# A two-block network on one core: the first 27 weight units in another order, and the taps of a 31-tap convolution summed in PSUM

## What is computed

```
u = rmsnorm(h, g_mix);  z = u @ w_in
zq, zkv, zg, zc, zm = split(z)               # queries, 6 x 2 groups of keys/values, gates, conv input, merge gates
kc, vc = compress(kv[0]), compress(kv[1])    # windows of 32 tokens, stride 16: gelu(flat(blocks + pos) @ w1) @ w2
o_c, o_s, o_w = attention of q over (kc, vc), (kv[2], kv[3]), (kv[4], kv[5])
y_a = (g0 * o_c + g1 * o_s + g2 * o_w) @ w_o_nsa     # g = sigmoid(zg)
c = c_val * sigmoid(c_gate)                  # the two halves of zc, 512 channels each
c = silu(layernorm(causal_dwconv(c, conv_w, conv_b)))       # 31 taps per channel
y_b = c @ w_conv_out + b_conv_out
h = h + (sigmoid(ga) * y_a + sigmoid(gb) * y_b) @ w_out
```

## Time and profile before

| | us |
|---|---|
| median of 3 runs | 2301.78 (2301.23 to 2301.85) |
| the profiled execution | 2300.76 |
| its span | 2298.8 |
| TensorE busy | 2156.7 (94%) |
| VectorE busy | 1082.4 (47%) |
| ScalarE busy | 863.0 (38%) |
| GpSimd busy | 925.4 (40%) |
| mean granted TensorE clock | 0.973 |

### The profile page before, as it was taken

The page is one execution under the profiler, slowest core; times in us unless marked ns, Lnnn a source line. Parts: engine busy times, 40 slices in busy tenths (PEclk is TensorE's granted clock), DMA queues, the critical chain, the costliest instruction groups (busy, mean ns, idle before and its releaser), DMA issues.

```text
span 2298.8 us, 25188 instructions
## 1 busy us (share of the span) xinstructions
PE 2156.7 (94%) x10138; PEld 1766.7 (77%) x10138; DVE 1082.4 (47%) x1665; ACT 863.0 (38%) x1344; POOL 925.4 (40%) x415
## 2 busy tenths in 40 slices
PE   7449999999999999989999999999899999999996
PEld 6437777778888888777777888888788788888875
DVE  3996666535552423556654423222553245222145
ACT  4123444434442335444443423223532234233243
POOL 4242222344444444522215444443654454444452
PEclk9779999999999999999999999999999999999998
DMA  4122111223333233211112233232223223333321
GB/s 151 55 92 65 47 45 48 73 92 102 101 92 101 93 105 105 64 56 56 46 37 93 92 101 101 92 101 92 93 71 103 90 75 101 93 100 97 96 90 49
DMA packets 53252, 192.73 MB, mean 84 GB/s; under 512 B 5904, under 2 KB 6032, under 8 KB 53136
## 3 DMA queue, kind: packets, MB, share of 16 engines
q1 hardware_dynamic: 52704, 189.55, 26.4%
q10 hardware_dynamic: 432, 1.57, 0.2%
HBM read 189.00 MB, written 2.10 MB: 83 GB/s over the span
## 4 chain that ended last, share of the span: by engine, by line
PE 82%; DVE 12%; ACT 5%; issue 1%; POOL 0%; DMA 0%; DVEq 0%; ACTq 0%; POOLq 0%
PE ps L461 25%; PE ps L463 24%; PE ps L462 24%; DVE conv_acc L1044 4%; PE ps L625 1%; PE ps L605 1%; PE ps L864 1%; ACT w_hi L1646 1%; DVE ps L1553 1%; PE ps L617 1%; PE ps L524 1%; PE ps L882 1%; DVE resid L1558 1%; DVE tile_a L1312 1%; PE ps L517 1%
## 5 line engine op out<-in xcount | busy, mean ns | idle before, releaser
L425 POOL TENSOR_TENSOR w_lo<-w_raw,w_hi 128x1024 fp32r<-128x1024 f32 x353 | 855.4, 2425 | 1303.8 <-ACT w_hi L1646 1303.8
L461 PE MATMUL ps<-xg_hi,w_hi 128*128 128x512 f32 x1776 | 712.1, 401 | 38.1 <-POOL w_lo L425 17.1
L463 PE MATMUL ps<-xg_hi,w_lo 128*128 128x512 f32 x1776 | 697.2, 393 | 0.0
L462 PE MATMUL ps<-xg_lo,w_hi 128*128 128x512 f32 x1776 | 697.0, 392 | 0.0
L1646 ACT ACTIVATE w_hi<-w_raw 128x1024 fp32r<-128x1024 f32 x353 | 372.7, 1057 | 623.6 <-PE ps L463 615.0
L461 PEld LDWEIGHTS ps<-xg_hi,w_hi 128*128 128x128 f32 x1776 | 336.8, 190 | 107.6 <-issue 22.2
L463 PEld LDWEIGHTS ps<-xg_hi,w_lo 128*128 128x128 f32 x1776 | 336.2, 189 | 71.7
L462 PEld LDWEIGHTS ps<-xg_lo,w_hi 128*128 128x128 f32 x1776 | 337.2, 190 | 63.9 <-issue 0.2
L462 PE MATMUL ps<-h_lo,w_hi 128*128 128x512 f32 x688 | 267.9, 389 | 0.0
L463 PE MATMUL ps<-h_hi,w_lo 128*128 128x512 f32 x688 | 267.9, 389 | 0.0
L461 PE MATMUL ps<-h_hi,w_hi 128*128 128x512 f32 x688 | 267.9, 389 | 0.0
(11 more groups left out here) (303 smaller groups left out, 2335.2 us busy)
## 6 DMA issues: line engine op xcount, KB each, us to landing
w_raw<-in_weights SPq DMA_DIRECT2D x353, 512.0 KB, 3.5
resid<-in_x SPq DMA_DIRECT2D x4, 512.0 KB, 6.9
out_x<-resid SPq DMA_DIRECT2D x8, 256.0 KB, 2.0
p_raw<-in_p ACTq DMA_DIRECT2D x3, 512.0 KB, 3.6
vec<-in_vectors SPq DMA_DIRECT2D x1, 252.5 KB, 4.3
```

Source lines behind the costliest of these rows:

```text
L425: pool.tensor_tensor(w_lo[:, slot, :], w_raw[:, u % RAW, :], w_hi[:, slot, :].bitcast(F32), ALU.subtract).then_inc(w_ready, 1)
L461: pe.matmul(o, w, x, start=start, stop=False)
L462: pe.matmul(o, w, xl, start=False, stop=False)
L463: return pe.matmul(o, wl, x, start=False, stop=stop)
```

## The change

- **Order of units**: `cmp_in` (4), `glu` tiles 0 to 3, then 8 pairs of one compression unit and one projection unit: `hidden_k` with `glu` tiles 4 to 7, `hidden_v` with the two keys and the two values. Then `q0`, `cmp_out`, `gates`. The packing of the weights follows. The group of five at the start is now `cmp_in` and the first `glu` tile.
- **Banks**: new ones for these units; the compression's sums lie in banks 4 and 5, its transposed hidden tiles both in bank 6, and both transposed value tiles, one after the other, in bank 3, so that the second transpose waits for `vv_lo` of the first (`s_kv["lo"]` of 4).
- **Taps**: the sum of every channel tile is in bank 7 (`taps(count)`). 62 lie ahead of attention in pieces of 2 to 14; 62 beside it, two in each slot, the second behind `pt_lo`. LayerNorm's additions move to the slots (0, 1), (4, 0) and (7, 3).
- **Gates**: their sigmoid goes into `ln_sum` instead of `sq`, and the transpose of the gates moves behind the first scores.
- **Start**: x in five pieces of 1, 1, 2, 2 and 2 chunks; ACT issues the 8 columns of `vec` with the first gain and the first half of unit 0, SP the second half; ACT and POOL split unit 0 by halves and TensorE starts on the first; the rest of `vec` comes behind x; a token activation stands ahead on ACT; TensorE multiplies `ones` by `ones` 8 times ahead of its first wait.
- `blk_lo` moves to another place in SBUF.

```diff
-    stage("glu", 8)
     stage("cmp_in", 4)
-    stage("cmp_hidden", 8)
-    stage("keys", 2)
+    stage("glu", 4)
+    stage("hidden_k", 8)
+    stage("hidden_v", 8)
+    stage("q0", 1)
     stage("cmp_out", 1)
-    stage("values", 2)
     stage("gates", 1)
-    stage("q0", 1)
...
+def glu_unit(t):
+    U = layout_units()
+    return U["glu"] + t if t < 4 else U["hidden_k"] + 2 * (t - 4) + 1
+def hidden_unit(kv, i):
+    return layout_units()[("hidden_k", "hidden_v")[kv]] + 2 * i
+def kv_unit(n):
+    return layout_units()["hidden_v"] + 2 * n + 1
...
+    for i in range(4):
+        bank[U["cmp_in"] + i] = i
+    for t in range(8):
+        bank[glu_unit(t)] = (4, 5, 6, 0, 1, 2, 3, 0)[t]
+    for n in range(4):
+        bank[kv_unit(n)] = (1, 2, 3, 0)[n]
+    bank[U["q0"]], bank[U["gates"]] = 2, 0
...
             load_x(0)
-            sp.dma_start(vec[:], vectors).then_inc(vec_loaded, 16)
-            load(0)
+            sp.dma_start(w_raw[:, 0, UW // 2:UW], weights[0, :, UW // 2:UW]).then_inc(w_loaded[0], 16)
             load_x(1)
+            load(1)
             load_x(2)
             load_x(3)
-            for u in range(1, U["end"]):
+            load_x(4)
+            sp.dma_start(vec[:, DC:NVEC], vectors[:, DC:NVEC]).then_inc(vec_loaded, 16)
+            for u in range(2, U["end"]):
...
+            for half in range(2):
+                cols = slice(half * UW // 2, (half + 1) * UW // 2)
+                pool.wait_ge(first_hi if half == 0 else w_hi_ready, 1)
+                pool.tensor_tensor(w_lo[:, 0, cols], w_raw[:, 0, cols], w_hi[:, 0, cols].bitcast(F32),
+                                   ALU.subtract).then_inc(first_ready if half == 0 else w_ready, 1)
...
+            pe.wait_ge(c_dve, 4)
+            for _ in range(EARLY_IDLE):
+                pe.matmul(ps[:, 0, 0:P], ones[:], ones[:], start=True, stop=True)
...
+            for t in range(1, 4):
+                unit(glu_unit(t))
+            for i in range(4):
+                hidden(0, i)
+                unit(glu_unit(4 + i))
+            for n in range(4):
+                hidden(1, n)
+                unit(kv_unit(n))
+                if n == 0:
+                    hidden_turn(0)
             hidden_turn(1)
-            unit(U["keys"] + 1)
+            values_turn(0)
+            unit(U["q0"])
+            values_turn(1)
...
+            def values_turn(j):
+                pe.wait_ge(bank_free, kv_unit(2 + j) + 1)
+                if j:
+                    pe.wait_ge(s_kv["lo"], 4)
...
+            def taps(count):
+                for n in range(tapped[0], tapped[0] + count):
                     ct, k = divmod(n, CONV_TAPS)
-                    acc, src, w = conv_acc[:, ct, :], glu[:, ct, k:k + S], vcol("conv_w", n)
-                    if ct == CT - 1:
-                        acc = ps[:, NB, :]
+                    acc, src, w = ps[:, NB, :], glu[:, ct, k:k + S], vcol("conv_w", n)
...
+            blocks(0, "pos_k")
+            glu_tile(0)
+            blocks(1, "pos_v")
+            block_low(0)
+            dve.wait_ge(bank_free, glu_unit(1) + 1)
+            taps(2)
+            block_low(1)
+            glu_tile(1)
+            taps(14)
+            glu_tile(2)
+            taps(14)
+            dve.wait_ge(bank_free, glu_unit(5) + 1)
+            glu_tile(3)
+            taps(4)
+            keys(0)
             hidden_low(0)
+            taps(6)
+            keys(1)
+            taps(8)
+            dve.wait_ge(bank_free, kv_unit(1) + 1)
+            kv_scaled(2, T2[:, 0:1, :])
+            taps(8)
+            kv_scaled(3, T2[:, 1:2, :])
             hidden_low(1)
+            taps(EARLY_TAPS - 56)
+            values_low(0)
+            query_scaled(0)
+            query_low(0)
+            values_low(1)
...
-                    if tap < CT * CONV_TAPS:
-                        taps(tap, tap + 1)
-                    elif tap < CT * CONV_TAPS + 3:
-                        ln_add(tap - CT * CONV_TAPS + 1)
+                    if tapped[0] < CT * CONV_TAPS:
+                        taps(1)
...
                         head_low(A1, event(b) + i, i)
+                    if tapped[0] < CT * CONV_TAPS:
+                        taps(1)
...
+            act.dma_start(vec[:, 0:DC], vectors[:, 0:DC]).then_inc(gain_loaded, 16)
+            act.dma_start(w_raw[:, 0, 0:UW // 2], weights[0, :, 0:UW // 2]).then_inc(first_loaded, 16)
+            act.wait_ge(c_dve, 4)
+            act.activation(token[:, 13:14], eps_col[:], ACT.Copy).then_inc(c_act, 1)
...
+            highs(glu_unit(0) + 1 + RING)
+            highs(glu_unit(1) + 1 + RING)
+            block_high(0)
+            glu_sigmoid(0)
+            highs(glu_unit(2) + 1 + RING)
+            block_high(1)
+            highs(glu_unit(3) + 1 + RING)
+            glu_sigmoid(1)
...
+            highs(kv_unit(0) + 1 + RING)
+            keys(0)
+            hidden_high(0)
+            highs(kv_unit(1) + 1 + RING)
+            keys(1)
```

More of the change, by code:

```diff
@@ L116, in bank_table @@
     bank = {}
[L117 to L121, removed]
+    for i in range(4):
[5 more added lines that the diff above has]
+    bank[U["q0"]], bank[U["gates"]] = 2, 0
+    for u in range(U["pairs"], U["w_out"]):
+        bank[u] = u % 2
     embeds = {U[f"ple{n}"] + i for n in range(3) for i in range(2)}
@@ L265, in build @@
             stat = sb("stat", [P, 3, 2, QB], scope=att)
+            with ExitStack() as early:
+                blk_lo = sb("blk_lo", [P, 2, 16, 2 * NC1], F32R, early)
             pt_hi = sb("pt_hi", [P, 2, S], F32R, att)
@@ L545, in _, with hidden @@
             group(u0, 7, DC, ready=prepared(0))
-            for u in range(u0 + GROUPS[u0], U["cmp_hidden"]):
-                unit(u)
+            def hidden(kv, i):
+                uu = hidden_unit(kv, i)
+                if i == 0:
+                    pe.wait_ge(s_cmp["lo"], kv + 1)
+                weights_here(uu)
+                for c in range(4):
+                    o = ps[0:2 * NC1, 4 + kv, 0:2 * P]
+                    xh, xl = blk_hi[:, kv, 4 * i + c, :], blk_lo[:, kv, 4 * i + c, :]
+                    wh, wl = (w[:, uu % RING, c * 2 * P:(c + 1) * 2 * P] for w in (w_hi, w_lo))
+                    mm = three(o, xh, wh, xl, wl, i == 0 and c == 0, i == 3 and c == 3)
+                mm.then_inc(unit_done, 1)
@@ L554, in hidden_turn @@
                 mm.then_inc(s_cmp["turned"], 1)
[L556 to L568, removed]
@@ L583, in _, with gates_turn @@
             mm.then_inc(unit_done, 1)
[L584 to L587, removed]
+            unit(U["gates"])
+            def gates_turn():
+                pe.wait_ge(s_gate["sig"], 1)
                 for tb in range(QB):
[L589 to L594, removed]
+                    mm = pe.transpose(ps[:, 4, tb * 32:(tb + 1) * 32], ln_sum[0:32, tb * P:(tb + 1) * P], ident[0:32, 0:32])
+                mm.then_inc(s_gate["turned"], 1)
             def head_scores(A, s, qi, terms):
@@ L1045, in taps, with glu_tile, blocks @@
                     ins.then_inc(s_mrg["conv"], 1)
[L1048 to L1051, removed]
+                tapped[0] += count
+            def glu_tile(i):
+                u, v = glu_unit(2 * i), glu_unit(2 * i + 1)
                 scaled(u, T[:, i % 2:i % 2 + 1, :], s_glu["t"])
-                scaled(u + 1, bank(u + 1), s_glu["t"])
+                scaled(v, bank(v), s_glu["t"])
                 dve.wait_ge(s_glu["t"], 2 * i + 2)
                 dve.wait_ge(s_glu["sig"], i + 1)
[L1056 to L1075, removed]
+                dve.tensor_tensor(glu[:, i:i + 1, PAD:PAD + S], T[:, i % 2:i % 2 + 1, :], bank(v), ALU.mult).then_inc(bank_free, 2 if i < 2 else 4)
+            def blocks(kv, pos):
                 for g in range(2):
@@ L1728, in _ @@
-            act.wait_ge(s_cmp["out"], 4)
-            copy_hi(kc_hi[:], kc_f[:], s_cmp["khi"])
-            copy_hi(vc_hi[:], vc_f[:], s_cmp["khi"])
-            highs(U["values"] + 2 + RING)
-            highs(U["gates"] + 1 + RING)
-            taken(U["gates"])
-            act.activation(sq[:, 0, :], T[:, 0, :], ACT.Sigmoid).then_inc(s_gate["sig"], 1)
+            values_high(0)
             def query_high(p):
@@ L1741, in _ @@
             query_high(0)
-            for j in range(2):
-                act.wait_ge(s_kv["turned"], j + 1)
-                for hd in range(2):
-                    cols = slice(hd * HD, (hd + 1) * HD)
-                    copy_hi(vv_hi[:, hd, j, :, cols], ps[:, 6 - j, :].rearrange("p (a b) -> p a b", b=P)[:, :, cols], s_kv["hi"])
+            values_high(1)
+            highs(U["cmp_out"] + 1 + RING)
+            act.wait_ge(s_cmp["out"], 4)
+            copy_hi(kc_hi[:], kc_f[:], s_cmp["khi"])
+            copy_hi(vc_hi[:], vc_f[:], s_cmp["khi"])
+            highs(U["gates"] + 1 + RING)
+            taken(U["gates"])
+            act.activation(ln_sum[:], T[:, 0, :], ACT.Sigmoid).then_inc(s_gate["sig"], 1)
             def exps(A, e, par, st, pr, qi, b):
```

197 lines of the change are left out of this document (112 added, 85 removed).

## The result

The changed kernel takes 2236.76 us (median of 4 runs, 2233.05 to 2239.36), the kernel before 2301.82 on the same chip: a ratio of 0.971 [0.968, 0.973], 65 us less. 2233.2 was forecast, in a range of 2223 to 2252. The profiled execution took 2233.05 us, the one before 2300.76: 67.7 less, where the sum of terms says 68.55. Runs of one kernel differ by 6 us here.

A forecast was written before the change was run, and what follows sets the result against it. VectorE's lateness ahead of attention, from convolution taps held beside POOL, was taken as the bound. Terms 5.4 + 62.3 + 7.05 - 3.8 - 0.9 - 1.5 = 68.55 us off 2300.76 gave 2232.2, plus 1.0 for the median: 2233.2 (2223 to 2252).

The forecast's parts named there:

- the check from below: Attention's start added up from TensorE's own items, first matmul to gates: 127.5 us, 70 earlier than 197.45.
- 1, the first matmul: Kernel start: first matmul at 7.0 us instead of 12.36, gain 5.4 us (4.5 to 6.5).
- 2, the waits: Ahead of attention, TensorE's waits on compression blocks' low parts, `hid_lo`, split weights, `tile_a` and `vv_lo` go: 62.3 us gained.
- C: Weight supply holds the unit pairs, as ACT takes splits behind sigmoids that wait for VectorE: 2243 us, chance 0.09.
- 3, the clock: Low-clock stretches behind waits ahead of attention go, half the start's too: gain 7.05 us (5 to 8), 0.85 at the start.
- 4, the new wait: Second value transpose: TensorE waits for `vv_lo` of the first, loss 3.8 us (0 to 7), plus 0.9 for low clock.
- 5, attention: Attention: 33 more taps beside it, delays taken up in the wait for `pt_hi`; loss 1.5 us (0 to 10).
- Two of the signs named: In attention: VectorE busy over 75%, and TensorE's waits not over 5 us.
- 6, gates and LayerNorm: Gates' sigmoid behind the first scores and LayerNorm's moved additions cost nothing; the sigmoid, if uncovered, 1 to 2 us.
- The rule weighed: VectorE competes with GpSimd only with two SBUF inputs or in a two-port mode; so early taps take 0.785 us.
- A: Early taps are held by POOL even with sums in PSUM, 25 us more on VectorE: 2258 us, chance 0.04.
- E: The mixed stage of short and long units never gets the high clock, slower than before: 2324 us, chance 0.02.

The follow-up runs named there:

- light second taps: The changed kernel with 29 of the 31 second taps in attention replaced by a one-element memset: 2232.64 us, 0.969 of the kernel before.

## Why the prediction was right, step by step

**The sum.** Up to attention the terms make 70.05 us and 67.8 came. Of the 2.2 missing, 2.1 stand at the end of the first group, 39.6 us where the check from below has 37.5: the first matmul was 0.6 late, and the group took 32.0 us and not 30.5. Attention took 3.3 us more, where the sum has 1.5. That the profiled execution still comes within 1 us of the sum is luck: behind attention, where nothing changed, it is 3.1 us shorter than the one before (TensorE is busy for 1811.8 us and not 1814.7, with the same 8316 matmuls). The changed kernel's second profile does not have these 3 us: 1876.0 there, against 1875.0 before and 1871.9 in the first.

**What bounds.** VectorE's lateness in the first stretch, and taps blocked beside POOL: shown from both sides, by one half of the change at a time.

**1, the first matmul.** 7.64, not 7.0; the gain is 4.7, inside 4.5 to 6.5 (8.15 in the second profile, and 7.7 to 8.1 in the experiments with this start). ACT had waited 0.46 us for the first half of unit 0 when it copied it at 5.45, and POOL had split it by 7.5. The working ended at 7.5, and the 0.5 that I took off for smaller pieces was not there: they landed at 5.4, not at 4.4.

**2, the waits.** 62.3 forecast, and all of it went. No unit behind the first one waits for weights up to attention, against C. C's mechanism is real all the same: with the taps in SBUF it is where most of the lateness comes out (15.6 us).

**3, the clock.** The four stretches behind waits went. At the start I counted 0.85 gained, and 1.0 was lost: 13 low matmuls in the profile (8 in the second one), where before has 8. The step asked whether a pause of 2 us would lose the high level; in this execution the eight idle matmuls never reached it. With 13 of them the first eviction comes 2.6 us earlier (1.9 against the second profile).

**4, the new wait.** 3.8 forecast, 3.3 measured, and it ends at `vv_lo` as the list says: VectorE begins the second glu tile 16.7 us after the first group's end (17.5 in the list), its `vv_lo` at 80.6 and ends it at 81.3 (81.7). TensorE's list is added up wrongly: its items make 77.5, not 77.9. TensorE stood there 78.2 us after the group, so the slip came out near the truth. The low clock behind the wait cost the whole of 1.6 (8 matmuls x 0.2) and 3.0 in the second profile, not 0.9.

**5, attention.** 1.5 forecast. The stretch from the masks to the first eviction of the mix is 226.4 us before, 229.7 after, and 228.8 with light second taps. With the low stretches taken out (6.6, 6.8 and 6.8 us lost by the granted clock) that is 219.8, 222.9 and 222.0. So the second taps cost 0.9, and attention as a whole is 3.1 longer. TensorE's waits hold 1.8 of that (1.2 on `ln_sum`, 0.6 on `prob_s`); the rest stays open. The step had the wrong cover, too: the taps go into the wait for scores more than into that for `pt_hi`. Two of the signs named failed: VectorE is 72% busy there, not over 75%, and TensorE's waits there make 8.8 us, not under 5 (7.0 before).

**6, gates and LayerNorm.** One wait of 1.2 us on `ln_sum` stands in the profile, which no row of before has; I had nothing, or 1 to 2 uncovered.

**The rule weighed** ("SBUF — State Buffer", section "SBUF: two separate sides" of the Trainium skill) is borne out: 116 taps with the sum in PSUM between 740 and 757 ns, through all of POOL's splits; with the sum in SBUF up to 2939. A is out. So is E: the pairs of long and short units ran at the high level, 0.99 over the stretch, with the one low stretch behind the new wait.

**What the forecast did not have** is a low stretch inside attention. In the changed kernel it begins at 170.5. The windows (columns as in the earlier trace rows):

```profile
168.00:170.00 2.00, 1.78 (x27) 1.72 (x27) 1.86 (x5) 0.35 (x2) 0.00 (x0) 1.00 0.13 53
170.00:172.00 2.00, 2.00 (x8) 1.43 (x6) 1.04 (x3) 0.41 (x1) 0.00 (x0) 0.65 0.00 0
172.00:174.00 2.00, 2.00 (x10) 1.53 (x10) 0.09 (x1) 0.00 (x0) 0.00 (x0) 0.50 0.03 8
```

Until 177 the clock is at 0.50, which costs 3.4 us. It stands behind the second compressed scores, 32 columns wide, which follow a wait of 0.52 us. It is not bound to the change: the kernel before has one, half as long, behind later compressed scores, at 333 us, the changed kernel's second profile has none at 170, and the one with light second taps has it. One profile of the kernel with the block ahead of the scores has none in attention before 326, yet its time is the same. Whether the short wait or the thin matmuls bring it stays open. Such stretches, there in one execution and not in the next, go with the spread of the runs: the granted clock is 0.986 in the fastest execution of the changed kernel (2233) and 0.982 in the slowest (2239). The median lies 3.7 above the profiled run, where I had put 1.0, and its executions have the lower clock.

## What to carry to other kernels

- When a chain of VectorE's adds runs beside GpSimd, try the accumulating operand in PSUM: here 1155 ns a tap became 750 and the other engine's work got shorter too. It was worth 30 us in the old order without any other change.
- Short units that need a fresh result of VectorE belong between long ones that need nothing; and work that nobody waits for belongs behind the result that TensorE waits for, as the four moved taps show (5.4 us).
- Idle matmuls at the start pay only if the clock rises during them and is still high at the first real one. Look at their own durations: eight, all of 421 ns, brought nothing; 13, the last of them of 274 ns and ended 1.5 us ahead, brought the first group's eviction forward by 1.9 to 2.6 us.
- A sum that fits to 1 us can do so by luck. Compare it stretch by stretch, the unchanged stretches too.

## What was not expected of the hardware

The level of TensorE's clock after a pause: behind the 13 idle matmuls it was still 2.4 GHz after 1.49 us of idle time; after 2.75, 2.94, 3.08 and 3.26 us it fell, and each time not within the pause but 0.2 to 1.7 us behind the start of the next matmul. And a fall without such a pause: at 170.5 us TensorE had been 89% busy over the two microseconds before, with a wait of 0.52 us and 32-column matmuls, and fell to 1.2 GHz for some 6.5 us.

Contention between VectorE and GpSimd is paid on both sides: a split of 2.39 us took 2.65 to 2.77 beside SBUF taps, and was still 2.39 beside PSUM taps.
